# A layer with 32 experts on one core: the expert weights in 2 MB transfers, 16 KB in one piece per partition

## The reference, cut to what matters

```python
x = x + mix                                   # the mixer's output
xn = rmsnorm(x, norm_ffn)                     # gain norm_ffn, one per feature
h = xb @ w_up[e] + b_up[e]                    # w_up[e]: 1024 x 2048, 8 MB
act = h_glu * sigmoid(1.702 * h_glu) * (h_lin + 1.0)   # both halves of h clamped at 7
y = act @ w_down[e] + b_down[e]               # w_down[e]: 1024 x 1024, 4 MB
```

## Time and profile before

| | |
|---|---|
| median of 3 runs | 1161.96 us (1161.11 to 1162.8) |
| the profiled execution | 1162.26 us, its span 1160.1 us |
| PE busy | 1120.2 us, 97% |
| PE weight loads busy | 446.4 us, 38% |
| DVE busy | 364.7 us, 31% |
| ACT busy | 147.0 us, 13% |
| DMA | 431.39 MB, mean 372 GB/s |
| mean granted TensorE clock | 0.989 |

### The profile page before, as it was taken

One profiled execution on the slowest core, in us unless ns is written; L12 is line 12 of the kernel. 1 busy time (PEld: TensorE's weight loads), 2 busy tenths in 40 slices (PEclk: granted clock), 3 DMA queues, 4 the chain that ended last, 5 costly groups with the idle time before them and its releaser, 6 DMA issues.

```text
span 1160.1 us, 12274 instructions
## 1 busy us (share of the span) xinstructions
PE 1120.2 (97%) x5152; PEld 446.4 (38%) x5153; DVE 364.7 (31%) x526; ACT 147.0 (13%) x290; POOL 8.4 (1%) x21
## 2 busy tenths in 40 slices
PE   6999995999999999999999999999999999999995
PEld 4888873333333333333333333333333333333321
DVE  1354503133333333333332222223333333333324
ACT  3121112111111111111111111111111111111111
POOL 1000000000000000000000000000000000000001
PEclk9999997999999999999999999999999999999997
DMA  7576742999999999999999999999999999999992
GB/s 246 175 278 220 254 167 93 416 416 416 416 418 416 418 416 418 416 417 417 417 417 417 417 418 417 417 417 418 416 417 417 417 417 417 417 416 417 416 413 103
DMA packets 94925, 431.39 MB, mean 372 GB/s; under 512 B 8531, under 2 KB 27955, under 8 KB 61813
## 3 DMA queue, kind: packets, MB, share of 16 engines
q1 hardware_dynamic: 94436, 430.48, 92.0%
q10 hardware_dynamic: 432, 0.10, 0.0%
HBM read 427.00 MB, written 3.48 MB: 371 GB/s over the span
## 4 chain that ended last, share of the span: by engine, by line
PE 80%; DMA 2%; DVE 1%; issue 0%; ACT 0%; POOLq 0%; POOL 0%; ACTq 0%; DVEq 0%
PE bank L979 39%; PE bank L998 19%; PE bank L1014 8%; PE bank L953 7%; PE bank L990 3%; DMA ring_a<-in_w_down 2%; PE bank L961 2%; PE bank L971 1%; PE bank L1027 0%; DVE h_tok L1235 0%; POOLq L822 0%; DVE h_tok L1279 0%; DVE hb L1210 0%; ACT h_rows L1173 0%; DVE av L1227 0%
## 5 line engine op out<-in xcount | busy, mean ns | idle before, releaser
L979 PE MATMUL bank<-ring_a,xs 128*64 128x512 f32 x1376 | 325.8, 600 | 2.0 <-issue 1.2
L1235 DVE TENSOR_TENSOR h_tok<-h_tok,bank 128x1024 f32<-128x1024 f32 (+1 forms) x99 | 120.5, 1217 | 385.7 <-PE bank L1014 373.6
L979 PEld LDWEIGHTS bank<-ring_a,xs 128*64 128x64 f32 x1376 | 89.3, 136 | 191.7 <-issue 188.3
L998 PE MATMUL bank<-ring_a,av 128*64 128x512 f32 x688 | 158.5, 596 | 1.7 <-DVE av L1227 0.9
L979 PE MATMUL bank<-ring_b,xs 128*64 128x512 f32 x672 | 159.5, 600 | 0.1
L1014 PE MATMUL bank<-y_rows,spread 64*128 64x512 f32 (+1 forms) x384 | 106.8, 633 | 3.4 <-DVE h_tok L1235 2.6
L372 PE MATMUL bank<-xnt,w_ring 128*128 128x264 f32 x448 | 103.0, 391 | 1.6 <-DVE h_tok L712 1.0
L953 PE MATMUL bank<-x_tok,pick 128*64 128x512 f32 x384 | 89.8, 603 | 2.9 <-PEq L109 2.4
L372 PEld LDWEIGHTS bank<-xnt,w_ring 128*128 128x128 f32 x448 | 85.7, 193 | 16.4 <-DVE h_tok L712 1.2
L998 PEld LDWEIGHTS bank<-ring_a,av 128*64 128x64 f32 x688 | 47.1, 137 | 92.7 <-issue 87.6
L979 PEld LDWEIGHTS bank<-ring_b,xs 128*64 128x64 f32 x672 | 43.4, 136 | 93.3 <-issue 90.5
(11 more groups left out here) (170 smaller groups left out, 516.4 us busy)
## 6 DMA issues: line engine op xcount, KB each, us to landing
ring_a<-in_w_up SPq DMA_DIRECT2D x172, 1024.0 KB, 19.2
ring_a<-in_w_down SPq DMA_DIRECT2D x86, 1024.0 KB, 22.3
ring_b<-in_w_up SPq DMA_DIRECT2D x84, 1024.0 KB, 19.5
ring_b<-in_w_down SPq DMA_DIRECT2D x42, 1024.0 KB, 22.3
w_ring<-in_w_in SPq DMA_DIRECT2D x14, 1024.0 KB, 5.1
w_ring<-in_w_out SPq DMA_DIRECT2D x4, 1024.0 KB, 5.6
ring_a<-in_state_ret SPq DMA_DIRECT2D x1, 2048.0 KB, 11.1
out<-ring_a SPq DMA_DIRECT2D x1, 2048.0 KB, 11.4
```

The costliest lines, as they stand in the source:

```text
L979: mm = pe.matmul(bank[half * CAP:(half + 1) * CAP, H + b, :], x, src[:, half * FF + b * 512:half * FF + (b + 1) * 512], start=(j == 0), st ...
L998: mm = pe.matmul(bank[half * CAP:(half + 1) * CAP, Y, :], av[:, 2 * i + k, :], src[:, k * D + half * 512:k * D + (half + 1) * 512], start= ...
L1235: tt(rows, rows, bank[0:m, C:C + 2, :], ALU.add).then_inc(comb_added, 1)
```

## The change

- A chunk of weights is 2 MB: `UC` is 4, `DC` is 2, and the ring has 9 slots of 2 MB, six in `ring_a` and three in `ring_b`, the same memory as before.
- In a chunk each partition holds rows that are neighbours in HBM: 2 rows of w_up, or 4 rows of w_down, 16 KB in one piece. So partition p of a chunk has features 2p and 2p+1 (up) or 4p to 4p+3 (down), where it had p and p+128.
- The other factor follows this order. The final ACT copy into `x_tok` writes even and odd features of each 256 apart; ACT's `h_out` writes each 512 columns so that neighbours land 128 elements (512 bytes) apart; the turned bias rows are taken with a stride of 4 elements; and norm_ffn is loaded a second time, as `g_pairs`, turned by two more transposes, and copied by one more ACT instruction into `vec[:, 96:104]`.
- PE's matmuls are as many and as large as before. It waits for a landing before every second `up` or `down`, and raises `mm_done` after every second.
- In phase 1 the 12 MB come as five transfers of 2 MB behind `w_ring` tiles 5, 7, 9, 11 and 13, and a sixth behind tile 16.

```diff
-    w_up_v = w_up[0].rearrange("e (k p) n -> e k p n", p=P)
-    w_down_v = w_down[0].rearrange("e (c k p) n -> e c p k n", p=P, k=2)
+    w_up_v = w_up[0].rearrange("e (c p k) n -> e c p (k n)", p=P, k=2)
+    w_down_v = w_down[0].rearrange("e (c p k) n -> e c p (k n)", p=P, k=4)
...
+                sp.dma_start(g_pairs, norm_ffn[0].rearrange("(c n) -> c n", c=4)).then_inc(rows_in, 16)
...
-                            pe.wait_ge(rows_in, 80)
-                            turn(bank[:, 7, 0:96], rows[0:96, :], 96).then_inc(rows_t, 1)
+                            pe.wait_ge(rows_in, 16 * 6)
+                            turn(bank[:, 7, 0:96], rows[0:96, :], 96)
+                            for pair in range(2):
+                                mm = turn(bank[:, 7, 96 + 4 * pair:100 + 4 * pair], g_pairs[:, pair:2 * P - 1 + pair:2], 4)
+                            mm.then_inc(rows_t, 1)
...
-                    mm = turn(bank[:, 6, j * E:(j + 1) * E], b_up_sb[:, j * P:(j + 1) * P], E)
+                    at = j // 4 * 4 * P + j % 4
+                    mm = turn(bank[:, 6, j * E:(j + 1) * E], b_up_sb[:, at:at + 4 * P - 3:4], E)
...
-                    nc.scalar.activation(x_tok[0:n, c, :], h_tok[0:n, c, :], ACT.Copy, scale=small[0:n, 9 + c:10 + c])
+                    nc.scalar.activation(x_tok[0:n, c, :].rearrange("p (c k q) -> p c q k", k=2, q=P),
+                                         h_tok[0:n, c, :].rearrange("p (c q k) -> p c q k", k=2, q=P),
+                                         ACT.Copy, scale=small[0:n, 9 + c:10 + c])
...
-                    for j in range(UC):
-                        s = place["u", n, j]
-                        pe.wait_ge(landed[s % RING], 16 * (s // RING + 1))
-                        up(n, j, ring(s))
+                    for j in range(KT):
+                        s = place["u", n, j // 2]
+                        if j % 2 == 0:
+                            pe.wait_ge(landed[s % RING], 16 * (s // RING + 1))
+                        mm = up(n, j, part(s, j))
+                        if j % 2:
+                            mm.then_inc(mm_done, 1)
...
                     for b in range(2):
-                        nc.scalar.activation(h_rows[:, b * 512:(b + 1) * 512], bank[:, H + b, :],
+                        nc.scalar.activation(h_rows[:, b * 512:(b + 1) * 512].rearrange("q (k p) -> q p k", k=4),
+                                             bank[:, H + b, :].rearrange("q (p k) -> q p k", k=4),
                                              ACT.Copy).then_inc(h_copied, 1)
```

More of the change, by code:

```diff
@@ L38 @@
 W = 256
-UC = 8
-DC = 4
+UC = 4
+DC = 2
 CPR = UC + DC
 FIRST = CPR
-RING = 18
+RING = 9
 TOK = [(0, 128), (128, 128), (256, NS)]
@@ L81, in hybrid_layer @@
         h_tok = sb("h_tok", [P, CT, D])
[L82 removed]
+        vec = sb("vec", [P, 104])
         pick = sb("pick", [P, CT, CAP])
@@ L141, in hybrid_layer @@
             state1 = h_tok[:, 1, 512:1024].rearrange("p (h n) -> p h n", h=HEADS)
+            g_pairs = k_tok[0:4, 0, 0:2, :].rearrange("p h e -> p (h e)")
             nc_t = sb("nc_t", [P, HEADS, 2 + NS])
@@ L293, in _ @@
                     if j >= 5:
-                        k = j - 5
-                        if k == 6:
+                        k = (j - 5) // 2
+                        if j == 11:
                             sp.wait_ge(bu_psum, 1)
-                        elif k == 8:
+                        elif j == 13:
                             sp.wait_ge(summed, 5)
-                        elif k == 10:
+                        elif j == 15:
                             store_states(sp)
-                        if k < 10:
+                        if j % 2 and k < 5:
                             sp.dma_start(ring_a[:, k, :], chunk_src(stream[k])).then_inc(landed[k], 16)
-                        elif k > 10:
+                        elif j == 16:
                             sp.wait_ge(state_out, 16)
-                            sp.dma_start(ring_a[:, k - 1, :], chunk_src(stream[k - 1])).then_inc(landed[k - 1], 16)
+                            sp.dma_start(ring_a[:, 5, :], chunk_src(stream[5])).then_inc(landed[5], 16)
                 sp.wait_ge(state1_out, 16)
@@ L909, in _ @@
                         sp.wait_ge(mm_done, s - RING + 1)
-                    sp.dma_start(chunk_dst(stream[s][0], ring(s)), chunk_src(stream[s])).then_inc(landed[s % RING], 16)
+                    sp.dma_start(ring(s), chunk_src(stream[s])).then_inc(landed[s % RING], 16)
                     if s == FIRST:
@@ L980, in up @@
                                            src[:, half * FF + b * 512:half * FF + (b + 1) * 512],
-                                           start=(j == 0), stop=(j == UC - 1))
-                    mm.then_inc(mm_done, 1)
+                                           start=(j == 0), stop=(j == KT - 1))
+                    return mm
                 def turn_h(n):
@@ L999, in down, with part @@
                                            src[:, k * D + half * 512:k * D + (half + 1) * 512],
-                                           start=(i == 0 and k == 0), stop=(i == DC - 1 and k == 1))
-                    mm.then_inc(mm_done, 1)
+                                           start=(i == 0 and k == 0), stop=(i == KT // 2 - 1 and k == 1))
+                    return mm
+                def part(s, j):
+                    return ring(s)[:, j % 2 * 2 * FF:(j % 2 + 1) * 2 * FF]
                 def combine(n, c):
@@ L1062, in downs @@
                         pe.wait_ge(y_copied, n)
[L1063 to L1066, removed]
+                    for i in range(KT // 2):
+                        s = place["d", n, i // 2]
+                        if i % 2 == 0:
+                            pe.wait_ge(landed[s % RING], 16 * (s // RING + 1))
+                        mm = down(i, part(s, i))
+                        if i % 2:
+                            mm.then_inc(mm_done, 1)
                         if i == 0 and n < E - 1:
@@ L1095, in overflow @@
                         pe.wait_ge(landed[j], k * 16 + landings(j) + 16)
-                        up(n, j, ring(j))
+                        up(n, 2 * j, part(j, 0))
+                        up(n, 2 * j + 1, part(j, 1)).then_inc(mm_done, 1)
                     turn_h(n)
@@ L1100, in overflow @@
                         pe.wait_ge(landed[UC + i], k * 16 + landings(UC + i) + 16)
-                        down(i, ring(UC + i))
+                        down(2 * i, part(UC + i, 0))
+                        down(2 * i + 1, part(UC + i, 1)).then_inc(mm_done, 1)
                     for c in range(CT):
```

21 lines of the change are left out of this document (10 added, 11 removed).

## The result

| | before | after |
|---|---|---|
| median of 4 runs | 1162.38 us (1161.11 to 1162.86) | 1175.77 us (1175.27 to 1176.26) |
| span of the profiled execution | 1160.1 us | 1173.7 us |
| ratio to before | | 1.0117, 95% interval 1.0099 to 1.0134 |

The account below looks back on a forecast made before the run. PE's instruction sequence was taken to bound the experts, DMA only their last 35 us. Terms 13.6 + 0.9 - 2.4 + 0.5 = +12.6 us on a span of 1160.1 led to a forecast of 1174.8 us, range 1160 to 1184.

Parts of the forecast that it names:

- PE's sequence bounds the experts, DMA the last 35 us: Whole expert phase: PE's own instructions set 29.29 us per expert; the stream, at 30.17, lives on a 12 MB lead.
- The gain of 2.4 us at the end: Last experts: a stream at 434 GB/s, 28.99 us per expert, removes PE's waits for landings, -2.4 us.
- the fourth rival: Weight stream stays at 417 GB/s despite the change; about 1175 us as forecast, no separate chance, counted in the forecast.
- Scattered write, 1049 ns from the one row with a 64-byte step: ACT's h_out copies: 1049 ns instead of 595, taken from bias_up, so 0.454 us more per 512 columns.
- Cover of 0.47 us, so 31 waits of 0.44: Before turn_h(1) to turn_h(31): the copy pair grows by 0.91 us, 0.47 is covered, PE waits 13.6 us in all.
- Once 0.9 without cover: Before ups(1), just behind h_out(0): the longer copies have no cover there, 0.9 us once.
- Bias transposes, 0.5: 16 bias-row transposes on PE's path: strided reads cost between 0 and 1.2 us more, taken as 0.5.
- Final copy to `x_tok`, nothing: End of phase 1: three ACT copies grow 0.91 us each, hidden by DVE with 0.5 us to spare; no cost.
- Ring and phase 1's queue, nothing: 2 MB slots and loads behind w_ring tiles: stream doesn't run dry; at worst 2.3 us lost once in the queue, taken as nothing.
- The rival of a free write: h_out's scattered writes cost nothing: 1160.1 us, or 1156.4 with free bias transposes and larger tail gain; 12%.
- that of a doubled price: h_out's 512-byte step twice as bad as 64: a pair of 3.8 us, 2.2 us wait per expert, about 1233; 6%.
- the stream as the bound: Phase 2's weight stream decides below 411 GB/s; at 400 the kernel would end near 1188 us; 5%.

Follow-up runs that it names:

- the step probe: Kernel before with h_out's copies in eight ways, four experts each: SBUF writes or PSUM reads at several steps; writes 1040 to 1115 ns at 16 bytes and more.
- Two engines side by side: Changed kernel, but ACT makes the first of h_out's two scattered copies and DVE the second, at the same time: 1160.97 us, ratio 0.9995.

## Why the prediction was right, step by step

The forecast of 1174.8 us was 1.0 us low. The mechanism was right: a scattered write on ACT, 31 times beyond its cover. That the sum is so near is in part luck, since its errors cancel: against the ledger, the 31 waits were put 0.9 us too dear and the gain at the end 0.3 too large, the step in expert 1 was put 1.5 too cheap and phase 1 0.6 too cheap, and 0.5 less (the first gather and the remainder) was not foreseen. Its steps:

- **PE's sequence bounds the experts, DMA the last 35 us.** Right: the changed kernel without the scattered write has the old period exactly; the stream's rate moved by 2.4% and the period not at all. But it says too little: with 7.7 us less for PE per expert, the kernel before gained only 1.1 us, so its stream is a bound almost as near.
- **The gain of 2.4 us at the end.** 2.1 by the ledger; the reason given, that the stream would be faster than PE, was wrong. It does 29.47 us per expert and not 28.99. The lead of 12 MB (30 us) carries the 0.18 us per expert that it is short, and in the changed kernel PE is slower still. The sum did not hang on the figure, as the fourth rival had said.
- **Scattered write, 1049 ns from the one row with a 64-byte step.** 1082 ns in the changed kernel, and the step probe shows that 64 and 512 bytes cost alike. The pair was put at 1.99 us and takes 1.96.
- **Cover of 0.47 us, so 31 waits of 0.44.** 31 of 0.41, 12.7 us instead of 13.6. The step probe confirms the cover: pairs of 1.89, 1.96 and 2.01 us cost what they have above 1.55 us, which is 1.08 + 0.47. Two engines side by side, with dearer copies and no loss, agree. The prediction puts the idle of 0.81 us down to PE's change of tile form, which no run here tests by itself; in the timeline it is the `down` pass that stands beside the copies, and the figure is the same by either reading.
- **Once 0.9 without cover.** The wait grew by 0.8, but a half clock of 1.6 us behind it was missed. That term was mis-sized: 2.4 instead of 0.9 in the profiled execution. In the kernel before, a wait of 1.23 us at this place was followed by no fall of the clock, and the prediction didn't ask what one of 2 us might do.
- **Bias transposes, 0.5.** 0.92 us (2.10 against 1.18): PE pays for reading SBUF with a step of 16 bytes as ACT does for writing, nearly double, and the nearer end was the upper one. The experiments agree: 1.18 in the kernels that read the rows in order, 2.10 in those that read them with the step. The phase as a whole came 1.07 us later, but by so much it also differs between profiles of the same code.
- **Start, nothing.** PE's first projection pass begins at 17.77 us, before the change at 17.96.
- **Final copy to `x_tok`, nothing.** The three now take 5.75 us from 188.68 to 194.43, and DVE ends at 195.17. Hidden, with 0.7 us to spare; 0.5 was forecast.
- **Ring and phase 1's queue, nothing.** No run that has a fast enough stream shows a cost above what phase 1 differs between profiles. But the kernel with 2 MB steps and the old pieces shows that this holds only there: 4.7 us.

The rival of a free write fell by 487 ns per copy, that of a doubled price by the probe, and the stream as the bound by 427 GB/s against the 411 from which it would have decided.

## What to carry to other kernels

An order that makes the pieces of a transfer longer must be made good by an engine somewhere, so first ask what the transfer's rate is worth: here 18.5 us for a kernel that waits for its stream, but only 2.1 for this one. Then look for what the waiting engine does meanwhile: in the kernel before the change, the time from the reordering engine's end to the start of the instruction that waits for it is the cover, and what sticks out of it is paid once per round. The releaser that a row names doesn't tell whether there was a wait; an idle longer than before an instruction that waits for nothing does. And where an order must be changed on the way from PSUM to SBUF, let ACT read with the step and write in order.

## What the runs showed of the hardware

- ACT writes SBUF at 594 ns for 512 columns in order, 632 at a step of 8 bytes, and 1040 to 1115 at 16, 64 and 512 bytes. It reads PSUM at 594 to 595 ns with a step of 2, 4, 16 or 128 elements.
- PE takes 1.18 us for 16 transposes of 32x128 whose rows it loads from SBUF in order, and 2.10 us when it loads them with a step of 16 bytes.
- While DVE makes a scattered copy at the same time, ACT's takes 1286 ns instead of 1082, and DVE's 1271.
- Queued HBM loads run at 417 GB/s with pieces of 8 and 4 KB and at 427 with 16 KB, whether the former come in transfers of 1 or 2 MB.
- The same idle of 2.05 us on PE was followed by 1.2 GHz in one kernel's profile and not in another's.
